# A routing stage on one Trainium2 core: two of four weighted one-hots per unit built by ScalarE instead of VectorE

## The reference, cut to what matters

```python
v1, i1 = lax.top_k(s1, PEER_TOPK)
v2, i2 = lax.top_k(s2, PEER_TOPK)
sc, j = lax.top_k(cand, PEER_TOPK)
idx = (jnp.take_along_axis(i1, j // PEER_TOPK, axis=-1) * PEER_KEYS
       + jnp.take_along_axis(i2, j % PEER_TOPK, axis=-1))
g = jax.nn.softmax(sc, axis=-1)
act = jax.nn.gelu(jnp.einsum('thkd,td->thk', u_tab[idx], xb), approximate=False)
return jnp.einsum('thk,thkd->td', g * act, v_tab[idx])
```

## Time and profile before

| | us |
|---|---|
| median of three runs | 4860.73 (4858.03 to 4862.85) |
| the profiled execution | 4847.97 |
| its span, first to last instruction | 4846.3 |
| busy over the whole span: PE | 4326.4 |
| DVE | 3032.4 |
| ACT | 969.1 |
| POOL | 1260.3 |

### The profile page before, as it was taken

One profiled execution on the slowest core, in us unless ns is written; L12 is line 12 of the kernel. 1 busy time (PEld: TensorE's weight loads), 2 busy tenths in 40 slices (PEclk: granted clock), 3 DMA queues, 4 the chain that ended last, 5 costly groups with the idle time before them and its releaser, 6 DMA issues. The chain is left out here.

```text
span 4846.3 us, 48883 instructions
## 1 busy us (share of the span) xinstructions
PE 4326.4 (89%) x16974; PEld 2666.9 (55%) x16974; DVE 3032.4 (63%) x6385; ACT 969.1 (20%) x1863; POOL 1260.3 (26%) x969
## 2 busy tenths in 40 slices
PE   8996686989999987888887988869999999999988
PEld 5554453665555545666663766654545455444534
DVE  1002351458777767989881487766889777877743
ACT  1112221111101104555541122220000000000023
POOL 0000031014444442333320000004444444444410
PEclk9998788999999997878878999989999999999999
DMA  4443496769999988978858777749999999999941
GB/s 166 144 146 103 143 320 280 279 245 422 379 386 391 374 337 279 343 286 308 331 218 322 291 256 258 239 149 417 419 404 410 419 419 419 415 415 412 412 184 58
DMA packets 363495, 1477.73 MB, mean 305 GB/s; under 512 B 38338, under 2 KB 178418, under 8 KB 242706
## 3 DMA queue, kind: packets, MB, share of 16 engines
q0 software_dynamic: 119872, 824.76, 42.4%
q1 hardware_dynamic: 193874, 625.13, 34.8%
q10 hardware_dynamic: 49536, 25.17, 1.7%
HBM read 1369.00 MB, written 115.38 MB: 306 GB/s over the span
## 5 line engine op out<-in xcount | busy, mean ns | idle before, releaser
L2552 POOL DMA_INDIRECT ex_uv<-in_uv,idx x768 | 1169.7, 1523 | 1706.2 <-DVE ex_acc L2609 1512.5
L2593 DVE CUSTOM_DVE_ANT_0 ex_uv<-ex_uv,ex_xp 128x1024 f32<-128x1024 f32 x768 | 912.8, 1222 | 290.6 <-DMA ex_uv<-in_uv,idx 243.4
L2609 DVE SCALAR_TENSOR_TENSOR ex_acc<-ex_uv,ex_wt,ex_acc 128x1024 f32<-128x1024 f32 x768 | 943.5, 1282 | 10.8 <-DVE C L893 3.2
L392 PE MATMUL proj_psum_acc<-proj_w,aT_later 128*128 128x385 f32 x2304 | 748.8, 487 | 7.7 <-DMA proj_w<-in_w_in 7.7
L2807 PE MATMUL exp_psum_dn<-exp_dn_big,exp_dn_gg 128*128 128x512 f32 x1536 | 685.1, 596 | 28.7 <-DVE exp_dn_gg L2763 28.6
L2798 PE MATMUL exp_psum_dn<-exp_dn_xT,exp_dn_big 128*128 128x384 f32 x2048 | 683.2, 487 | 6.9 <-DMA exp_dn_big<-in_ud 6.9
L392 PEld LDWEIGHTS proj_psum_acc<-proj_w,aT_later 128*128 128x128 f32 x2304 | 437.0, 190 | 319.1 <-DMA proj_w<-in_w_in 7.9
L2798 PEld LDWEIGHTS exp_psum_dn<-exp_dn_xT,exp_dn_big 128*128 128x128 f32 x2048 | 390.0, 190 | 306.4 <-issue 69.5
L2807 PEld LDWEIGHTS exp_psum_dn<-exp_dn_big,exp_dn_gg 128*128 128x128 f32 x1536 | 291.0, 191 | 379.1 <-issue 351.8
L301 PE MATMUL proj_psum_acc<-proj_w,aT 128*128 128x385 f32 x1152 | 377.4, 488 | 4.5 <-DMA proj_w<-in_w_in 2.6
L301 PEld LDWEIGHTS proj_psum_acc<-proj_w,aT 128*128 128x128 f32 x1152 | 218.5, 190 | 159.4 <-issue 5.1
(11 more groups left out here) (460 smaller groups left out, 4241.7 us busy)
## 6 DMA issues: line engine op xcount, KB each, us to landing
proj_w<-in_w_in SPq DMA_DIRECT2D x48, 1540.0 KB, 10.4
rt_w<-in_w_q SPq DMA_DIRECT2D x36, 2048.0 KB, 8.4
exp_dn_big<-in_ud SPq DMA_DIRECT2D x128, 512.0 KB
exp_dn_big<-in_vd SPq DMA_DIRECT2D x128, 512.0 KB
scratch_z<-proj_zs SPq DMA_DIRECT2D x216, 192.5 KB, 2.0
rt_w<-in_w_br_m SPq DMA_DIRECT2D x18, 2048.0 KB, 9.0
rt_w<-in_w_br_f SPq DMA_DIRECT2D x18, 2048.0 KB, 8.9
rt_w<-in_w_out SPq DMA_DIRECT2D x18, 2048.0 KB, 8.0
```

The source lines that it names most:

```text
L392: mm = pe.matmul(acc[j % SLOTS][:, 0:CW], aT[:, k, t * P:(t + 1) * P], w[:, u % U, k, :], start=(k == 0), stop=(k == KD - 1))
L2552: pool.indirect_dma_start(self.uv[:, slot, :], None, self.uv_tab, bass.IndirectOffsetOnAxis(ap=self.idx[:, at:at + 1], axis=0)).then_inc(s ...
L2593: dve.tensor_tensor_reduce(self.uv[:, slot, 0:D], self.uv[:, slot, 0:D], self.xp[:], 1.0, 0.0, ALU.mult, ALU.add, self.dot[:, g % 2, j:j + ...
L2609: dve.scalar_tensor_tensor(out=self.acc[:, j % 2, :], in0=self.uv[:, slot, D:2 * D], scalar=self.wt[:, g % 2, j:j + 1], in1=self.acc[:, j ...
```

## The change

ScalarE takes over `oh1` of the tokens 2 and 3 of every unit (`BY_ACT`). It makes each by two activations, a first Abs(iota - row number) and a second Relu(weight - weight * that), which gives the weight where the row number matches and 0 elsewhere. `act_turn` therefore also stores the negated row numbers and the negated weights, by two more copies with a factor of -1, and waits for its own three copies. VectorE keeps `oh2` and the `oh1` of tokens 0 and 1.

`act_one(u)` holds the four activations, with a wait of ScalarE on itself between the two Abs and the two Relu. ScalarE calls it two units ahead (`LEAD`): each `act_clear(u)` becomes `act_unit(u)`, which first makes the one-hots of unit u+2 and then clears unit u. Units 0 and 1 are made right after the first `act_turn`. TensorE waits for one more semaphore before a unit.

```diff
+    BY_ACT = (2, 3)
+    LEAD = 2
-        self.selT = st.sb("so_selT", [P, 2, 3, P])
+        self.selT = st.sb("so_selT", [P, 2, 5, P])
+        self.off_set, self.one_act, self.sel_set = st.sems("so_off_set so_one_act so_sel_set")
 # dve_one
-        for t in range(U):
+        for t in [t for t in range(U) if t not in self.BY_ACT]:
 # pe_spread
         pe.wait_ge(self.one, u + 1)
+        pe.wait_ge(self.one_act, u + 1)
 # act_turn
-        act.copy(self.selT[:, d % 2], self.banks[item % 2][:, 0:3 * P].rearrange("p (s n) -> p s n", s=3)
-                 ).then_inc(self.cleared, 1)
+        bank = self.banks[item % 2][:, 0:3 * P].rearrange("p (s n) -> p s n", s=3)
+        for s in range(2):
+            act.mul(self.selT[:, d % 2, 3 + s, :], bank[:, 2 * s], -1.0).then_inc(self.sel_set, 1)
+        act.copy(self.selT[:, d % 2, 0:3], bank).then_inc(self.cleared, 1)
+        act.wait_ge(self.cleared, item + 1)
+        act.wait_ge(self.sel_set, 2 * d + 2)
+
+    def act_one(self, act, u):
+        if u >= self.UNITS:
+            return
+        U, (d, r), slot = self.U, divmod(u, self.PER_TILE), u % self.DEEP
+        if u == 0:
+            act.wait_ge(self.iota_set, 2)
+        if u >= self.DEEP:
+            act.wait_ge(self.spread, self.item(u - self.DEEP) + 1)
+        for t in self.BY_ACT:
+            n = r * U + t
+            ins = act.activation(self.oh1[:, slot, t, :], self.iota[:], ACT.Abs, bias=self.selT[:, d % 2, 3, n:n + 1])
+        ins.then_inc(self.off_set, 1)
+        act.wait_ge(self.off_set, u + 1)
+        for t in self.BY_ACT:
+            n = r * U + t
+            ins = act.activation(self.oh1[:, slot, t, :], self.oh1[:, slot, t, :], ACT.Relu,
+                                 bias=self.selT[:, d % 2, 2, n:n + 1], scale=self.selT[:, d % 2, 4, n:n + 1])
+        ins.then_inc(self.one_act, 1)
+
+    def act_unit(self, act, u):
+        self.act_one(act, u + self.LEAD)
+        self.act_clear(act, u)
 # stage_route, ScalarE
                 if turned(t):
                     so.act_turn(act, t - so.FROM)
+                    if t == so.FROM:
+                        for u in range(so.LEAD):
+                            so.act_one(act, u)
...
                 for u in spread(t, 0, 14):
-                    so.act_clear(act, u)
+                    so.act_unit(act, u)
```

## The result

The changed kernel takes 4877.39 us (median of nine runs, 4866.57 to 4883.43), the kernel before 4862.02 in the same comparison (nine runs, 4854.02 to 4868.06). The ratio is 1.0031, 95% interval 1.002 to 1.0041: slower by 10 to 20 us.

What follows compares the result with a forecast made beforehand. TensorE with short stalls bounds t = 2 to 4, VectorE t = 5. Iterations +4.2, +3.25, +1.65, -3.95 and clock +1.5 total +6.6 us: median 4867.3, range 4853 to 4884.

Steps and rivals of the forecast that it cites:

- ACT dearer: Rival: ScalarE reads both pointers one after the other and waits cost more: +9.6 us and more; chance 0.28.
- a: ScalarE's time for one unit's four activations: 1.36 us, inside 1.29 to 1.47; 0.1 us in it is 3.3 us.
- A unit on DVE: One unit's one-hots on VectorE: two of four tensor_scalars go, -0.51 us, to 1.12.
- A unit on ACT: One unit's four new activations on ScalarE, with self-wait and Relu's second pointer: 1.36 us.
- A burst: Groups of units where TensorE waits for ScalarE's one-hots and clears: units 4 to 9 +2.85, +2.85, +1.3 us.
- The stall before unit 14: TensorE's wait after the branch matmuls, 4.47 us in t = 3: shrinks to about 3 us; -0.51 us at unit 14.
- Start of t = 2: After act_turn, its added copies and the one-hots of units 0 to 2 delay the branches by 4.4 us.
- End of an iteration: Units 20 to 23: out matmuls +1.25 us, but net -0.5 through earlier adds; next start +1.8.
- Last iteration: t = 5: VectorE's 11 units -5.6, units 88 to 91 -0.3, last four units +1.95: -3.95 us.
- Clock: TensorE's granted clock after idling: gain at the shorter stall, loss in bursts; +1.5 us net, between -5 and +6.
- Tables: Rival: Abs or Relu needs another table on ScalarE, two switches of 1.28 us a unit: +246 us, 5107; chance 0.04.
- Other side: Rival: VectorE was the bound everywhere that counts, ScalarE's one-hots fit its idle time: -12 to -17 us, 4846; chance 0.09.

Runs made afterwards that it cites:

- the reordered kernel: Changed kernel with ScalarE first clearing a burst, then making the next burst's one-hots; deeper buffers, units 0 to 3 by VectorE: median 4838.24 us, ratio 0.9951.
- gain_only: Kernel before, with VectorE making oh1 of tokens 0 and 1 alone, nobody those of tokens 2 and 3: median 4837.04 us, ratio 0.9949.

## Why the prediction was right, and where it was not

The median lies in the range (4853 to 4884) and on the side that was forecast, and the mechanism is the one that was priced. The size was short: +6.6 forecast, +9.6 in the stretch and +10 to +20 by the ratio. The rival "ACT dearer", a from 1.45 up, is the case that came: a is 1.51. With it came one of the prediction's own signs of being wrong, "an ACT unit beyond 1.5 us", and the outcome "slower", which had 0.37, not "same", which had 0.53. The forecast's own +6.6 lay under the limit of 9.7 us, below which it called a difference untellable, so that the sign came out right shows less than it seems. By the prediction's slope, 3.3 us for 0.1 in a, a = 1.51 makes +11.5 of the sum; 9.6 came, as other terms were off the other way.

- *By iteration* (turned picks to turned picks; t = 5, which has none, from its first unit to its last): +8.6, +3.8, +2.9, -5.8 for t = 2 to 5, forecast +4.2, +3.25, +1.65, -3.95 and the clock's +1.5 apart. Without the clock's term the miss is 4.4 in t = 2 and nothing in the other three together.
- *A unit on DVE*: 1.63 to 1.12 forecast; 1.11 measured.
- *A unit on ACT*: 1.36 forecast, 1.51 measured. The mis-sized term is Relu: from the start of the pair to what follows it lie 0.78 us, where the forecast's terms make 0.58. The groups after the change (ns min/median/max) have the Abs with one pointer and the Relu with two:

```profile
L2062 ACT ACTIVATE rt_so_oh<-rt_so_iota,rt_so_selT x192: 384/399/432, 2824.1 to 3274.2; 128x128 f32<-128x128 f32 x192
```
```profile
L2067 ACT ACTIVATE rt_so_oh<-rt_so_oh,rt_so_selT x192: 477/486/497, 2824.8 to 3275.0; 128x128 f32<-128x128 f32 x192
```

  The Relu is 0.087 longer. I had the second pointer as a bound, 0.18 for the pair, and took 0.07. That it is the pointer is my reading; function and source differ as well. The lower bound of a, 1.12, should have been 1.14 (1.01 + 0.13), which changes nothing here.

  The Trainium skill's budget ("ScalarE: Activation LUTs", Rules for kernel authors) made 1.63 a unit and +15 us as an estimate. Its unit came a little nearer to 1.51 than my 1.36; its sum is nearer to the medians and farther from the stretch. It is right for the length of one (0.41 against 0.399) and too high for a row of them, since the pitch of the Abs pair is 0.69 - 0.40 = 0.29. The Trainium skill's advice in the same section, to leave relu to VectorE, agrees with the changed order and not with the reordered kernel, whose median is 21 us under the one before.
- *A burst*: 8.4 forecast for units 4 to 9, 9.5, 8.7, 9.5 measured in t = 2 to 4 (in the first and last of these the last unit took 1.9 instead of 1.1, in t = 2 at a granted clock of 0.53). Units 10 to 13: 4.65 forecast, 4.8. The stall before unit 14: about 3 forecast, 2.9, and still on DVE. I had left out that the W store's issue stands before the next one-hots, 0.55 each.
- *Start of t = 2*: +4.4 forecast, +5.8 measured. Up to the first clear it is +5.0 (9.0 us after the first transpose before, 14.0 here): three sets of one-hots, which ran ahead of it as forecast but at 1.51 each, and the additional copies. The rest comes from units 2 and 3, which took 3.8 us at a granted clock of 0.50 after PE had waited. First clear before, first clear after, and those two units:

```profile
2808.75 0.62 ACT L2050 COPY rt_so_stage<-rt_psum_so 128x512 f32<-128x512 f32 x1
```
```profile
2833.73 0.56 ACT L2081 COPY rt_so_stage<-rt_psum_so 128x512 f32<-128x512 f32 x1
```
```profile
2834.44 4.02 PE L2036 MATMUL rt_psum_so<-rt_so_oh 128*128 128x128 f32 x16 [5.12 <-ACT rt_so_stage L2081]
```

- *End of an iteration*: out matmuls 5.7 after unit 20 forecast, 5.9 measured. From unit 20 to the next iteration's branches the forecast makes +1.3 (-0.5 and +1.8), +1.9 came, both times.
- *Last iteration*: -3.95 forecast, 99.5 for 105.2 us: -5.7.
- *Clock*: +1.5 forecast. It moved both ways: the branch matmuls took up to 1.1 us longer after PE had stood idle (15.0 us against 13.9 for the first 32 of t = 2), and units 14 and 15 took 2.3 instead of 3.8 and 3.4 in two of three iterations. In t = 2 to 4 the branch matmuls lost 3.9 and the last units of bursts 1.6; units 14 and 15 gave back 3.0 and the query matmuls 2.3. So these terms come to about nothing, not to +1.5.
- *Tables*: no new load; 11 in the stretch before and after. The Trainium skill ("ScalarE: Activation LUTs", Table sets) has relu and abs in every set, and the trace agrees with that.
- *Other side*: its mechanism exists, and I priced it at half. -12 to -17 against -26.4: I had kept two terms (units 16 to 19, the adds) at the value that ACT's cost leaves them. In gain_only units 16 to 19 alone gave 9.2 us where I had 3.4. And its condition, a under 0.36, was needless: a stays at 1.51 in the reordered kernel. My "or where ACT gets its work done ahead of the bursts" was the half that counts, and I gave it 0.09 without pricing it.

## What to carry to other kernels

An engine with half of its time idle is no free helper if its queue is in order and the helper's work stands between two links of another engine's chain: read its rate inside the burst (1.98 us against 0.93), not its share of the iteration. Put such work behind the burst, with buffers as deep as the next burst is long; nearly the same instructions then went from +10 to -25 us of stretch, 28 us of it by place and 7 by the start. A lead of one unit more didn't do it (+8.4), because each step still makes one before it clears one. And price a gain and its cost by themselves, one kernel with the gain alone and one with the cost alone: both were larger here (26 and 36 us) than their difference let one think.

## What was not expected of the hardware

- A 128 x 128 float32 activation on ScalarE takes 0.399 us in the median as Abs with one pointer operand and 0.486 as Relu with two; the two Relu of a unit span 0.88 us.
- The second attention stage, the same code in all ten profiles, takes 750 to 767 us on one core, and 749.9 and 762.0 in two executions of one program. Two profiles of the kernel before differ by 19.6 us of span (4846.3 and 4865.9), so differences of single profiles under 20 us say nothing of a change until the stretch is named.
